# The last modulation section computed by VectorE during gate and up

## The chip, the cores and the metric

The program runs on one core of a Trainium2 chip. The metric is the device time of one execution in microseconds. Engines: TensorE (PE; its weight loads are PEld), VectorE (DVE), ScalarE (ACT), GpSimd (POOL) and SyncE (SP), which here only issues DMAs. All data are fp32.

## The reference, cut to what matters

One block of a diffusion backbone over 640 tokens (128 of a prompt, 512 of a sample), width 2048, hidden width 5632. Two condition vectors, one for each group of tokens, give six modulation sections of 2048 columns:

```python
mod_ctx = jax.nn.silu(c_ctx) @ w_ada[l] + b_ada[l]
mod_lat = (jax.nn.silu(c) @ w_ada[l] + b_ada[l])[:, None, :]
...
sh1, sc1, g1, sh2, sc2, g2 = jnp.split(mod, 6, axis=-1)
h = x * (1 + sc1) + sh1
m, s_f, s_b = mixer(h, ...)                     # w_in, heads, pooling, w_out
x = layer_norm(ALPHA * x + g1 * m, ln1_g, ln1_b)
h = x * (1 + sc2) + sh2
gate, up = jnp.split(h @ w_gu, 2, axis=-1)
f = (jax.nn.silu(gate) * up) @ w_down
x = layer_norm(ALPHA * x + g2 * f, ln2_g, ln2_b)
```

The last section, g2, is used only behind the down product.

## The kernel before

The stages follow one another: a first part with sections sh1 and sc1; 33 units of w_in, between which the four heads and the pooling run (to 753 us); w_out; gate and up (from 984 to 2095 us); down and the last norm.

**Precision.** Every large product is done as three matmuls: ScalarE rounds a weight to `w_hi` (L977, L1210, L1312), VectorE or GpSimd subtracts to get the rest `w_lo` (L1377, L1666, L956), and TensorE does hi*hi, hi*lo and lo*hi.

**Modulation.** The other four sections (16 MB of `w_ada` each) are computed between the units of w_in. A row of 512 columns is four steps of four matmuls (`ada_step`, L2011: condition of 32 columns as stationary operand, 512 weight columns moving, fp32). A written-out order (`make_schedule`) has 9 places `SLOT` and 2 places `INNER` in each of the four heads; `with_modulation` fills each with a pair of steps until the 64 are used, at the end of the third head. The two `INNER` lie between two groups of outer products. At the next `SLOT` a row is summed over the four partial results: `adasum` (L2191) for a section kept as rows in DRAM (`mod_d`), `adacol` (L2198) for one kept as columns.

**Gate and up.** A block b is 128 hidden columns of gate and of up. The two first blocks are plain; the other 42 are done by a scheme of seven products in place of eight. A product is 24 matmuls of 320 columns (L2278 to L2280), numbered n from 16 to 309; its seven weights, called items 0 to 6 here, are made of four quarters A11, A12, A21, A22 of 128 x 1024. GpSimd forms four sums in a row for a block (L942, L945, L948, L951); item 2 is the last of them, items 3, 4 and 6 the others, and 0, 1 and 5 are quarters as loaded. ScalarE rounds an item (L1210), VectorE takes the rest (the split, L1666, `prod_rest`), and TensorE uses it four products later (four weight buffers). Each engine's queue is written in the order of n: VectorE at n does the sums of the product before (`post`, L1839 to L1858, and L1822), then the split of item n - 1. SyncE loads a quarter of the next block as soon as the split that frees its buffer is done: A12 behind item 2, A11 behind item 3, A21 behind item 4, A22 behind item 5, and stores a finished block in between. GpSimd's first sum waits for A21 and A22; its third and fourth also wait for the splits of items 0 and 1.

Of the kernel before, what the change touches and what calls it, by code (L numbers as in the profile page):

```python
# [20 lines left out]
ALU = mybir.AluOpType  # L21
# [130 lines left out]

def prod_of(n):

    return PLAIN + (n - N_PLAIN) // 7, (n - N_PLAIN) % 7
# [14 lines left out]
ADA = [(2, "row", 0), (4, "col", SC), (3, "col", SH), (5, "row", 1)]  # L170
# [7 lines left out]
N_ADA = 16  # L178
# [49 lines left out]
def with_modulation(flat):  # L228


    out, done, behind = [], 0, []
    for item in flat:
# [4 lines left out]
        if done < ADA_STEPS:  # L237
            out += [("ada", done // 4, done % 4), ("ada", done // 4, done % 4 + 1)]
            done += 2
            last = done // 4 - 1 if done % 4 == 0 else None  # L240
# [81 lines left out]
def backbone(nc, x_all, state_gla, w_ada, w_in_b, wa2, w_pool_l, w_out, w_gu_b, w_down, consts,  # L322
# [62 lines left out]
    group_sum = cols(C_SUM, 2)  # L385
    mod_col = cols(C_MOD, 64).rearrange("p (s k c) -> p s k c", s=2, c=2)
# [221 lines left out]
    down_gates = sem("down_gates")  # L608
    down_filled = sem("down_filled")
# [46 lines left out]
    def _(sp):  # L656
# [144 lines left out]
        for i in range(2, N_OUT):  # L801
# [3 lines left out]
            if i == 4:  # L805
                for x in range(2):
                    sp.wait_ge(spilled[x], 16 * n_out[x])
                    sp.wait_ge(drained[x], FILLS[x])
                sp.wait_ge(row_out, 16 * 8)
                load_gates(0)  # L810
# [59 lines left out]
        def load_down_rows(nb):  # L870

            if nb == 0:
                for x in range(2):
                    sp.wait_ge(hid_out[x], 16 * FB // 2)
                sp.wait_ge(prod_done, N_PROD)
                sp.wait_ge(xn_out, 16 * TT)
            else:
                sp.wait_ge(down_evac, TT * nb)
# [10 lines left out]

        for b in range(PLAIN + 1, FB):  # L890
            load_quad(b + 1, A12)
            load_quad(b + 1, A11)
            if b == PLAIN + 1:
                store_hid(0)
            store_hid(b - 2)
            load_quad(b + 1, A21)
            load_quad(b + 1, A22)
        load_down(0)
# [62 lines left out]
    def _(act):  # L961
# [7 lines left out]
        def split_in(u):  # L969
# [5 lines left out]
            elif u >= 3:  # L975
# [6 lines left out]
                             ACT.Silu).then_inc(cond_ready, 1)  # L982

# [329 lines left out]

        for n in range(9, N_PROD):
            b, i = prod_of(n)
            if n > N_PLAIN and i == 1:
                act.wait_ge(prod_done, n)
                act.wait_ge(gated, 2 * b - 2)
                nc.scalar.activation(post_a(b), prod_bank(n - 1), ACT.Copy).then_inc(first_copy, 1)
            if n - 1 < N_ITEM:  # L1320
# [45 lines left out]
    def _(dve):  # L1366
# [492 lines left out]

        for n in range(9, N_PROD + 1):  # L1860
# [6 lines left out]
            if n - 1 < N_ITEM:  # L1867
                prod_rest(n - 1)
            if n == 12:
# [123 lines left out]
    def _(pe):  # L1993
# [332 lines left out]

        for n in range(N_PLAIN, N_PROD):
            pe.wait_ge(prod_split, n - 3)
# [117 lines left out]
```

## Time and profile before

| | us |
|---|---|
| median of 3 runs | 2719.36 (2711.6 to 2723.58) |
| the profiled execution | 2721.88 |
| its span | 2720.1 |
| TensorE busy | 2643.3 (97%) |
| VectorE busy | 1424.9 (52%) |
| ScalarE busy | 898.4 (33%) |
| GpSimd busy | 652.8 (24%) |

The span runs from the first to the last instruction in the trace. Busy shares are means over stages with different limits. Where TensorE is busy all the time, the matmuls themselves are the limit; for any other engine it matters when it ends what TensorE waits for, not how busy it is. In the rows a bracket behind an instruction gives the idle time ahead of it and what ended it.

### The profile page before, as it was taken

Reading aid. Unit: us, or ns where it says so; the run is one execution under the profiler, and the core shown is the slowest. Engines: PE = TensorE matmul, PEld = TensorE weight load, DVE = VectorE, ACT = ScalarE, POOL = GpSimd, SP = SyncE. Lnnn points to the kernel's source line nnn. Section 1 sums busy time; section 2 is a strip of 40 time slices with the busy share of each in tenths; the row PEclk is TensorE's granted clock in tenths of the full one; section 3 lists DMA queues with packets and bytes.
Section 4 is the critical chain, followed back from the end, with each engine's and each line's share of the span. In section 5 each row is a group of like instructions: output and inputs, shape, how many; then the busy total and the mean of one; then the engine's idle time right before and its main releaser. Section 6 shows DMA issues by size and latency. Waiting matters only on the chain.

```text
span 2720.1 us, 37395 instructions
## 1 busy us (share of the span) xinstructions
PE 2643.3 (97%) x16040; PEld 2354.7 (87%) x16040; DVE 1424.9 (52%) x1680; ACT 898.4 (33%) x940; POOL 652.8 (24%) x218
## 2 busy tenths in 40 slices
PE   5999999998999999999999999999999999999997
PEld 3787877797988879999999999999999888888875
DVE  5323232346576457655555545555566354444578
ACT  4333333332311154333333333333333333333343
POOL 0000000000000001344443444344434333333440
PEclk9999999999999989999999999999999999999998
DMA  9775757422463142332233323332334645464566
GB/s 378 281 277 209 272 207 255 153 90 91 176 218 118 64 159 80 108 108 88 93 108 108 96 86 106 108 103 84 101 108 158 239 174 213 174 213 166 208 231 233
DMA packets 179384, 438.11 MB, mean 161 GB/s; under 512 B 9980, under 2 KB 25732, under 8 KB 173076
## 3 DMA queue, kind: packets, MB, share of 16 engines
q1 hardware_dynamic: 176916, 430.48, 45.4%
q10 hardware_dynamic: 2304, 5.24, 0.5%
q8 instruction: 127, 2.08, 0.3%
q14 instruction: 37, 0.30, 0.0%
HBM read 401.83 MB, written 33.85 MB: 160 GB/s over the span
## 4 chain that ended last, share of the span: by engine, by line
PE 62%; DVE 11%; DMA 10%; POOL 10%; issue 4%; ACT 3%; SPq 0%; POOLq 0%; ACTq 0%; DVEq 0%
PE ps L2355 6%; PE ps L2356 6%; PE ps L2357 6%; DMA raw_w<-w_gu_b 5%; PE ps L2278 5%; PE ps L2280 5%; PE ps L2279 5%; PE ps L2031 5%; PE ps L2033 5%; PE ps L2032 5%; POOL raw_w L945 3%; PE ps L2011 3%; DVE w_lo L1666 3%; POOL low L942 2%; POOL raw_w L948 2%
## 5 line engine op out<-in xcount | busy, mean ns | idle before, releaser
L1666 DVE TENSOR_TENSOR w_lo<-raw_w,w_hi 128x1024 fp32r<-128x1024 f32 x264 | 336.6, 1276 | 297.6 <-ACT w_hi L1210 294.7
L1210 ACT ACTIVATE w_hi<-raw_w 128x1024 fp32r<-128x1024 f32 x264 | 270.1, 1054 | 601.0 <-POOL raw_w L951 368.9
L2278 PE MATMUL ps<-x_hi,w_hi 128*128 128x320 f32 x1408 | 435.7, 309 | 1.0 <-DVE w_lo L1666 0.7
L2279 PE MATMUL ps<-x_lo,w_hi 128*128 128x320 f32 x1408 | 435.1, 309 | 0.0
L2280 PE MATMUL ps<-x_hi,w_lo 128*128 128x320 f32 x1408 | 435.1, 309 | 0.0
L942 POOL TENSOR_TENSOR low<-raw_w 128x1024 f32<-128x1024 f32 x41 | 103.7, 2528 | 1098.8 <-DMA raw_w<-w_gu_b 1058.7
L1801 DVE TENSOR_TENSOR x_lo<-low,x_hi 128x2560 fp32r<-128x2560 f32 (+2 forms) x55 | 221.3, 4027 | 262.6 <-ACT x_hi L1303 262.6
L2355 PE MATMUL ps<-w_hi,x_hi 128*128 128x512 f32 x880 | 343.8, 391 | 7.7 <-DVE w_lo L1932 2.8
L2356 PE MATMUL ps<-w_lo,x_hi 128*128 128x512 f32 x880 | 343.1, 390 | 0.0
L2357 PE MATMUL ps<-w_hi,x_lo 128*128 128x512 f32 x880 | 342.9, 390 | 0.0
L2278 PE MATMUL ps<-low_r,w_hi 128*128 128x320 f32 x1072 | 333.0, 311 | 1.5 <-DVE w_lo L1666 1.5
L2279 PE MATMUL ps<-low_r,w_hi 128*128 128x320 f32 x1072 | 332.2, 310 | 0.0
L2280 PE MATMUL ps<-low_r,w_lo 128*128 128x320 f32 x1072 | 332.1, 310 | 0.0
L2031 PE MATMUL ps<-x_hi,w_hi 128*128 128x320 f32 x1024 | 322.9, 315 | 1.8 <-DVE x_lo L1434 1.8
L2033 PE MATMUL ps<-x_hi,w_lo 128*128 128x320 f32 x1024 | 316.6, 309 | 0.0
L2032 PE MATMUL ps<-x_lo,w_hi 128*128 128x320 f32 x1024 | 316.5, 309 | 0.0
L956 POOL TENSOR_TENSOR w_lo<-raw_w,w_hi 128x2048 fp32r<-128x2048 f32 x45 | 212.5, 4723 | 352.5 <-ACT w_hi L1312 352.5
L2278 PEld LDWEIGHTS ps<-x_hi,w_hi 128*128 128x128 f32 x1408 | 264.4, 188 | 1.8 <-DVE w_lo L1666 1.3
L2279 PEld LDWEIGHTS ps<-x_lo,w_hi 128*128 128x128 f32 x1408 | 264.4, 188 | 0.0
L2280 PEld LDWEIGHTS ps<-x_hi,w_lo 128*128 128x128 f32 x1408 | 264.3, 188 | 0.0
L1377 DVE TENSOR_TENSOR w_lo<-raw_w,w_hi 128x2048 fp32r<-128x2048 f32 x48 | 110.0, 2291 | 262.8 <-ACT w_hi L977 262.7
L1312 ACT ACTIVATE w_hi<-raw_w 128x2048 fp32r<-128x2048 f32 x55 | 105.4, 1916 | 380.6 <-PE ps L2357 364.5
(238 smaller groups left out, 4362.9 us busy)
## 6 DMA issues: line engine op xcount, KB each, us to landing
raw_w<-w_gu_b SPq DMA_DIRECT2D x180, 512.0 KB, 5.6
low<-w_ada SPq DMA_DIRECT2D x68, 1024.0 KB, 6.9
raw_w<-w_down SPq DMA_DIRECT2D x55, 1024.0 KB, 5.2
low<-hidden_scratch SPq DMA_DIRECT2D x33, 1280.0 KB, 6.0
raw_w<-w_in_b SPq DMA_DIRECT2D x33, 1024.0 KB, 9.1
x_raw<-w_ada SPq DMA_DIRECT2D x25, 1024.0 KB, 15.2
raw_w<-w_out SPq DMA_DIRECT2D x16, 1024.0 KB, 5.1
hidden_scratch<-high SPq DMA_DIRECT2D x44, 320.0 KB, 5.9
```

Of the source, the lines that this page charges most:

```text
L1210: nc.scalar.activation(weight(0, w), src, ACT.Copy).then_inc(prod_hi, 1)
L1666: nc.vector.tensor_tensor(weight(1, n), src, weight(0, n).bitcast(F32), ALU.subtract).then_inc(prod_split, 1)
L1801: nc.vector.tensor_tensor(hid_slot(x_lo, j), hid_raw(j), hid_slot(x_hi, j).bitcast(F32), ALU.subtract).then_inc(hid_split, 1)
L2031: mm(out, wh, xh, start=first, stop=False)
L2032: mm(out, wh, xl, start=False, stop=False)
L2033: ins = mm(out, wl, xh, start=False, stop=last)
L2278: mm(out, wh, version(v, 0, k), start=first and k == 0, stop=False)
L2279: mm(out, wh, version(v, 1, k), start=False, stop=False)
L2280: ins = mm(out, wl, version(v, 0, k), start=False, stop=last and k == HK - 1)
L2355: mm(ps[:, (i + 7) % 8, :], xh, rh, start=begin, stop=False)
L2356: mm(ps[:, (i + 7) % 8, :], xh, rl, start=False, stop=False)
L2357: ins = mm(ps[:, (i + 7) % 8, :], xl, rh, start=False, stop=end)
```

## The change

Section 5 (g2) is no longer among the sections done between the units of w_in: 12 rows and 48 steps are left of 16 and 64. Since every third `SLOT` is now left empty, they still end with the third head. Section 5 is computed during gate and up: 8 groups of 256 columns, each 16 steps (one for every 128 rows of `w_ada`), one step every second product. A step is a load of 128 x 256 into one buffer (L928 of the new kernel), and on VectorE, behind the split of that product, two instructions that add the loaded tile times the condition to two running sums (`late_step`; a scalar_tensor_tensor, L1947, or a tensor_scalar at a group's start, L1949). Every 34 products TensorE sums a group over the partitions with four small matmuls (`sum_late`, running sums as stationary operand, ones moving), ScalarE copies the result, and SyncE stores it with four DMAs of one column.

```diff
+def late_at(n):
+    q, at = divmod(n - LATE_FROM, LATE_GAP)
+    return (q, at) if n >= LATE_FROM and q < N_LATE else (N_LATE, 0)
+def late_step_of(n):
+    q, at = late_at(n)
+    return KT * q + at // 2 if q < N_LATE and at % 2 == 0 and at < 2 * KT else None
...
-ADA = [(2, "row", 0), (4, "col", SC), (3, "col", SH), (5, "row", 1)]
+ADA = [(2, "row", 0), (4, "col", SC), (3, "col", SH)]
+LATE, LATE_FROM, LATE_W, LATE_GAP = 5, 26, 256, 34
+N_LATE = D // LATE_W
...
-N_ADA = 16
+N_ADA = 12
...
-        if done < ADA_STEPS:
+        seen += item[1] == 0
+        if done < ADA_STEPS and (item == INNER or seen % 3):
...
+        def late_traffic(n):
+            i = late_step_of(n + 2)
+            if i is not None:
+                if i:
+                    sp.wait_ge(late_used, i)
+                else:
+                    sp.wait_ge(cond_late, 1)
+                at = LATE * D + LATE_W * (i // KT)
+                sp.dma_start(late_stage, w_ada[P * (i % KT):P * (i % KT) + P, at:at + LATE_W]).then_inc(late_in, 16)
+            q, at = late_at(n - 1)
+            if q < N_LATE and at == 2 * KT + 1:
+                sp.wait_ge(late_row_done, q + 1)
+                for c in range(2):
+                    for half in range(LATE_W // P):
+                        to = LATE_W * q + P * half
+                        j = 4 * c + 2 * half
+                        sp.dma_start(mod_d[1, c, to:to + P], late_row[:, j:j + 1]).then_inc(late_out, 16)
         for b in range(PLAIN + 1, FB):
+            n = ITEMS + 7 * (b - PLAIN)
             load_quad(b + 1, A12)
+            late_traffic(n - 4)
             load_quad(b + 1, A11)
+            late_traffic(n - 3)
...
             load_quad(b + 1, A21)
+            late_traffic(n - 2)
             load_quad(b + 1, A22)
+            for i in range(-1, 3):
+                late_traffic(n + i)
...
+        def late_act(n):
+            q, at = late_at(n)
+            if q < N_LATE and at == 2 * KT + 1:
+                act.wait_ge(late_sum, q + 1)
+                if q:
+                    act.wait_ge(late_out, 16 * 4 * q)
+                nc.scalar.activation(late_row, ps[:, (n + 4) % 8, HALF:HALF + 8], ACT.Copy).then_inc(late_row_done, 1)
...
+        def late_step(n):
...
+            q, k = divmod(i, KT)
+            dve.wait_ge(late_in, 16 * (i + 1))
...
+            for c in range(2):
+                acc, by = cols(late_acc[c], LATE_W), cond_now[:, k, c:c + 1]
+                if k:
+                    ins = nc.vector.scalar_tensor_tensor(acc, late_stage, by, acc, ALU.mult, ALU.add)
+                else:
+                    ins = nc.vector.tensor_scalar(acc, late_stage, by, None, ALU.mult)
+            ins.then_inc(late_used, 1)
...
             if n - 1 < N_ITEM:
                 prod_rest(n - 1)
+            late_step(n)
...
+        def sum_late(n):
+            q, at = late_at(n)
+            if q == N_LATE or at != 2 * KT:
+                return
+            pe.wait_ge(late_used, KT * (q + 1))
+            if q:
+                pe.wait_ge(late_row_done, q)
+            for j in range(4):
+                at = late_acc[j // 2] + P * (j % 2)
+                ins = mm(ps[:, (n + 5) % 8, HALF + 2 * j:HALF + 2 * j + 2], cols(at, P), cols(C_ONES, 2),
+                         start=True, stop=True)
+            ins.then_inc(late_sum, 1)
         for n in range(N_PLAIN, N_PROD):
+            sum_late(n)
```

TensorE in the heads, at the sixth `SLOT` of a head, before: the end of a group of products with the states (64x256), a pair of steps (32x512, eight matmuls), a column sum (128x2), the next unit.

```order
L2161 MATMUL ps<-low 64x256 x2
L2166 MATMUL ps<-low 64x256 x2
L2161 MATMUL ps<-low 64x256 x2
L2166 MATMUL ps<-low 64x256 x2
L2011 MATMUL ps<-low,perm 32x512 x8
L2198 MATMUL ps<-perm,high 128x2 x4
L2031 MATMUL ps<-x_hi,w_hi 128x320
```

And in the new order, at the same place:

```order
L2254 MATMUL ps<-low 64x256 x2
L2259 MATMUL ps<-low 64x256 x2
L2254 MATMUL ps<-low 64x256 x2
L2259 MATMUL ps<-low 64x256 x2
L2284 MATMUL ps<-high,perm 2x512
L2124 MATMUL ps<-x_hi,w_hi 128x320
L2125 MATMUL ps<-x_lo,w_hi 128x320
```

The pair is gone; which sum stands here has shifted, since rows now end at other places.

VectorE in gate and up, from the split of item 2 to that of item 5, before (L1666 the splits, the others sums on finished products):

```order
L1666 TENSOR_TENSOR w_lo<-raw_w,w_hi 128x1024
L1857 TENSOR_TENSOR high<-ps,high 128x320
L1858 TENSOR_TENSOR high<-ps,high 128x320
L1666 TENSOR_TENSOR w_lo<-raw_w,w_hi 128x1024
L1822 TENSOR_TENSOR high<-high 128x320
L1666 TENSOR_TENSOR w_lo<-raw_w,w_hi 128x1024
L1839 TENSOR_TENSOR high<-ps,high 128x320
L1666 TENSOR_TENSOR w_lo<-raw_w,w_hi 128x1024
```

The same in the new order, in every second block (L1732 the splits, L1947 the new step):

```order
L1732 TENSOR_TENSOR w_lo<-raw_w,w_hi 128x1024
L1947 SCALAR_TENSOR_TENSOR perm<-perm 128x256 x2
L1923 TENSOR_TENSOR high<-ps,high 128x320
L1924 TENSOR_TENSOR high<-ps,high 128x320
L1732 TENSOR_TENSOR w_lo<-raw_w,w_hi 128x1024
L1888 TENSOR_TENSOR high<-high 128x320
L1732 TENSOR_TENSOR w_lo<-raw_w,w_hi 128x1024
L1947 SCALAR_TENSOR_TENSOR perm<-perm 128x256 x2
L1905 TENSOR_TENSOR high<-ps,high 128x320
L1732 TENSOR_TENSOR w_lo<-raw_w,w_hi 128x1024
```

Two steps stand between the split of item 2 and that of item 5; in the blocks between these there is one, behind item 3.

## Rows read from the trace of the kernel before

**Rows 1.** The page, busy time of each engine: us, share of the span, instructions.

```profile
PE 2643.3 (97%) x16040; PEld 2354.7 (87%) x16040; DVE 1424.9 (52%) x1680; ACT 898.4 (33%) x940; POOL 652.8 (24%) x218
```

**Rows 2.** Busy us by stretch (PE, PEld, DVE, ACT, POOL; TensorE's clock, DMA share, GB/s).

```profile
270.00:520.00 250.00, 249.32 (x1807) 201.33 (x1807) 84.34 (x135) 82.90 (x106) 0.75 (x1) 1.00 0.67 239
1100.00:2060.00 960.00, 959.96 (x6546) 959.69 (x6545) 522.77 (x624) 325.47 (x390) 417.04 (x156) 1.00 0.31 100
```

**Rows 3.** Timeline of TensorE, a pair of modulation steps (start, us, what) and what follows.

```profile
514.80 1.92 PE L2011 MATMUL ps<-low,perm 128*32 128x512 f32 x16
516.65 0.70 PE L2072 MATMUL ps<-low 64*128 64x256 f32 x2
```

**Rows 4.** The same, a row sum and what follows, then four column matmuls.

```profile
531.26 1.02 PE L2191 MATMUL ps<-high,perm 128*2 128x512 f32 x2 [0.88 <-DVE low L1619]
532.21 0.41 PE L2031 MATMUL ps<-x_hi,w_hi 128*128 128x320 f32 x1
...
288.07 1.05 PE L2198 MATMUL ps<-perm,high 128*128 128x2 f32 x8
288.99 0.40 PE L2031 MATMUL ps<-x_hi,w_hi 128*128 128x320 f32 x1
```

**Rows 5.** Timelines of VectorE and TensorE at the scores of a head.

```profile
303.15 0.82 DVE L1553 TENSOR_TENSOR low<-low 128x640 f32<-128x640 f32 x1
...
306.39 0.80 PE L2126 MATMUL ps<-low 128*64 128x64 f32 x20
```

**Rows 6.** Timeline of VectorE over one block of gate and up.

```profile
1309.20 1.23 DVE L1666 TENSOR_TENSOR w_lo<-raw_w,w_hi 128x1024 fp32r<-128x1024 f32 x1 [6.01 <-ACT w_hi L1210]
...
1318.77 0.49 DVE L1842 TENSOR_TENSOR high<-ps,high 128x320 f32<-128x320 f32 x1 [1.20 <-PE ps L2280]
...
1325.81 0.49 DVE L1851 TENSOR_TENSOR high<-high,ps 128x320 f32<-128x320 f32 x1 [1.10 <-PE ps L2280]
1326.33 1.00 DVE L1854 TENSOR_TENSOR high<-high 128x320 f32<-128x320 f32 x1
1333.35 1.23 DVE L1666 TENSOR_TENSOR w_lo<-raw_w,w_hi 128x1024 fp32r<-128x1024 f32 x1 [6.02 <-ACT w_hi L1210]
...
1336.42 0.48 DVE L1822 TENSOR_TENSOR high<-high 128x320 f32<-128x320 f32 x1
1336.82 1.22 DVE L1666 TENSOR_TENSOR w_lo<-raw_w,w_hi 128x1024 fp32r<-128x1024 f32 x1
...
1338.36 1.22 DVE L1666 TENSOR_TENSOR w_lo<-raw_w,w_hi 128x1024 fp32r<-128x1024 f32 x1
...
1343.41 0.49 DVE L1842 TENSOR_TENSOR high<-ps,high 128x320 f32<-128x320 f32 x1 [1.20 <-PE ps L2280]
```

**Rows 7.** Timeline of GpSimd, its four sums and the next start.

```profile
1321.21 2.42 POOL L942 TENSOR_TENSOR low<-raw_w 128x1024 f32<-128x1024 f32 x1 [13.20 <-DVE w_lo L1666]
1323.77 3.21 POOL L945 TENSOR_TENSOR raw_w<-raw_w 128x1024 f32<-128x1024 f32 x1
...
1329.75 2.41 POOL L951 TENSOR_TENSOR raw_w<-raw_w 128x1024 f32<-128x1024 f32 x1
1345.71 2.41 POOL L942 TENSOR_TENSOR low<-raw_w 128x1024 f32<-128x1024 f32 x1 [13.55 <-DMA raw_w<-w_gu_b]
```

**Rows 8.** Timelines of ScalarE (rounding) and SyncE (the last two quarters).

```profile
1332.26 2.01 ACT L1210 ACTIVATE w_hi<-raw_w 128x1024 fp32r<-128x1024 f32 x2 [8.90 <-POOL raw_w L951]
...
1338.07 1.86 SPq L827 DMA_DIRECT2D raw_w<-w_gu_b  x2
```

**Rows 9.** A group of VectorE by form: count, busy us, mean ns, idle before.

```profile
L1593 DVE SCALAR_TENSOR_TENSOR low<-low,perm,ps 128x256 f32<-128x256 f32 x56 | 26.9, 480 | 1.7
```

**Rows 10.** DMA issues: count, KB each, median us to landing.

```profile
raw_w<-w_gu_b SPq DMA_DIRECT2D x180, 512.0 KB, 5.6
low<-state_gla SPq DMA_DIRECT2D x8, 128.0 KB, 6.9
low<-w_pool_l SPq DMA_DIRECT2D x4, 256.0 KB, 3.0
```

More of the change, by code:

```diff
@@ L228, in with_modulation @@
 def with_modulation(flat):
-    out, done, behind = [], 0, []
+    out, done, behind, seen = [], 0, [], 0
     for item in flat:
@@ L385, in backbone @@
     group_sum = cols(C_SUM, 2)
+    late_acc = [C_COND + LATE_W * c for c in range(2)]
+    late_stage = cols(C_VEC, LATE_W)
+    cond_now = cols(C_VEC + LATE_W, 32).rearrange("p (k c) -> p k c", c=2)
+    late_row = cols(C_VEC + LATE_W + 32, 8)
     mod_col = cols(C_MOD, 64).rearrange("p (s k c) -> p s k c", s=2, c=2)
@@ L608, in backbone @@
     down_gates = sem("down_gates")
+    cond_late = sem("cond_late")
+    late_in = sem("late_in")
+    late_used = sem("late_used")
+    late_sum = sem("late_sum")
+    late_row_done = sem("late_row_done")
+    late_out = sem("late_out")
     down_filled = sem("down_filled")
@@ L808, in _ @@
                     sp.wait_ge(drained[x], FILLS[x])
-                sp.wait_ge(row_out, 16 * 8)
+                sp.wait_ge(row_out, 16 * 4)
                 load_gates(0)
@@ L876, in load_down_rows @@
                 sp.wait_ge(xn_out, 16 * TT)
+                sp.wait_ge(late_out, 16 * 4 * N_LATE)
             else:
@@ L982, in _ @@
                              ACT.Silu).then_inc(cond_ready, 1)
+        act.wait_ge(cond_ready, 1)
+        nc.scalar.activation(vec(V_COND, 32), vec(V_COND, 32), ACT.Silu).then_inc(cond_ready, 1)
         def in_rooted(t):
@@ L1319, in _ @@
                 nc.scalar.activation(post_a(b), prod_bank(n - 1), ACT.Copy).then_inc(first_copy, 1)
+            late_act(n)
             if n - 1 < N_ITEM:
@@ L1858, in post @@
                 nc.vector.tensor_tensor(a, prod_bank(m), a, ALU.add).then_inc(posted, 1)
+        def late_step(n):
+            if n == LATE_FROM - 4:
+                dve.wait_ge(cond_ready, 2)
+                dve.wait_ge(folded_s, 2 * HK)
+                dve.wait_ge(folded_v, 2 * HK)
+                nc.vector.tensor_copy(cond_now, vec(V_COND, 32).rearrange("p (k c) -> p k c", c=2)).then_inc(cond_late, 1)
+            i = late_step_of(n)
+            if i is None:
+                return
+            q, k = divmod(i, KT)
+            dve.wait_ge(late_in, 16 * (i + 1))
+            if i:
+                dve.wait_ge(late_used, i)
+            else:
+                dve.wait_ge(cond_late, 1)
+            if q and not k:
+                dve.wait_ge(late_sum, q)
+            for c in range(2):
+                acc, by = cols(late_acc[c], LATE_W), cond_now[:, k, c:c + 1]
+                if k:
+                    ins = nc.vector.scalar_tensor_tensor(acc, late_stage, by, acc, ALU.mult, ALU.add)
+                else:
+                    ins = nc.vector.tensor_scalar(acc, late_stage, by, None, ALU.mult)
+            ins.then_inc(late_used, 1)
         for n in range(9, N_PROD + 1):
@@ L2325, in bank_free @@
                 pe.wait_ge(posted, 4 * (b - PLAIN) + max(1, i - 2))
+        def sum_late(n):
+            q, at = late_at(n)
+            if q == N_LATE or at != 2 * KT:
+                return
+            pe.wait_ge(late_used, KT * (q + 1))
[6 more added lines that the diff above has]
+            ins.then_inc(late_sum, 1)
         for n in range(N_PLAIN, N_PROD):
+            sum_late(n)
             pe.wait_ge(prod_split, n - 3)
```

## The prediction

> **What bounds the kernel now.** I read the page's busy times first, then the busy times by stretch, then the waits, and then the timeline of each engine over one block of gate and up. TensorE is busy 2643 of 2720 us [rows 1]: a matmul taken from it counts in full wherever it has no idle time. It has none in the two stretches that the change touches: 249.3 of 250 us while the heads are computed, and 959.96 of 960 us in gate and up, at full granted clock [rows 2]. So time taken from TensorE in the first stretch is gained, and what is put into the second costs nothing only as long as nobody there gets later than TensorE.
>
> How late they are now is the question. In gate and up a block of seven products takes TensorE 24.64 us: the same VectorE sum, released by TensorE, stands at 1318.77 and 1343.41 [rows 6]. Beside it runs a second cycle, of the weights. When the split of item 5 is done (1338.36 + 1.22 = 1339.58), SyncE issues the last quarter of the next block (the second issue of its row, at 1339.60) [rows 6, 8]. It lands and GpSimd starts its four sums at 1345.71, 6.13 us later [rows 7]. In the block before they ran from 1321.21 to 1332.16, 10.95 us [rows 7]. ScalarE rounds item 2 from 1332.26 and VectorE splits it from 1333.35 to 1334.58 [rows 6, 8]; the splits of items 3, 4 and 5 and the sums between them stand in its queue right behind, without a gap, up to 1339.58. From split to split of item 2 that is 1333.35 - 1309.20 = 24.15 us, and from sums to sums 1345.71 - 1321.21 = 24.50 [rows 6, 7]. The cycle of the weights is thus as long as TensorE's, 0.1 to 0.5 us shorter. Its reserve: item 2, done at 1334.58, is wanted by the product that starts three products after the one that ended at 1325.8, so at 1325.8 + 3 x 3.52 = 1336.3, 1.7 us later [rows 6]. The busy shares hide this: VectorE is busy only 523 of the 960 us [rows 2].
>
> **The change, part by part.** The sum is made against the profiled execution (span 2720.1, time 2721.9 us), 2.5 us above the median of 2719.4.
>
> *Taken out of the heads.* 16 steps of matmuls go, which stand in pairs: a pair takes from 514.80 to 516.65, 1.85 us [rows 3]; 8 x 1.85 = 14.8. Four sums of a row go, each 531.26 to 532.21, 0.95 us [rows 4]: 3.8. Together 18.6 us. Pairs leave the third, sixth and ninth slot of each head, so something could come late that they had covered. The tightest place is the scores: VectorE ends its last factor at 303.97 and TensorE uses it from 306.39 [rows 5], 2.4 us of room against 1.85 taken out ahead of it. The pairs between the two groups of outer products stay. I cost exposed waits at 0, at most 8 x 1 us. The 16 MB read less here free DMA queues for which TensorE doesn't wait: nothing.
>
> *Put on TensorE.* Eight times, four small fp32 matmuls. The same form takes 288.07 to 288.99, 0.92 us [rows 4]: 7.4 us if TensorE is never waiting, and nothing where it waits in every block anyway. Each also waits for the last VectorE step, two products earlier. That step stands behind a split that only the product after this one needs, so it can hold TensorE by up to a product (3.5 us); the seven blocks around then run on the reserve so won. I put 3 us on it.
>
> *Put on VectorE.* 128 steps of two instructions of 256 columns, one step every second product, behind a split. The trace shows no such operation with both inputs in SBUF. With one in PSUM 256 columns take 480 ns [rows 9]; a plain product of 320 columns in SBUF keeps the queue for 1336.82 - 1336.42 = 0.40 us [rows 6], 0.32 for 256. I take 0.375 each, nearer to the row of the same memory, 0.75 for a step. Of TensorE's 7.04 us for two products that is little. For the weights' cycle it is not: of its 24.15 us, the stretch from the split of item 2 to that of item 5 is queue order on VectorE, and alternately two steps (behind items 2 and 4) or one (behind item 3) fall in it. So 1.5 steps a block, +1.1 us (0.95 to 1.45).
>
> *GpSimd's sums.* While GpSimd works, VectorE's operations with two SBUF inputs are not free: the 320-column product that took 0.48 at 1336.42, with GpSimd idle, took 1.00 at 1326.33, and the sum that GpSimd started at 1323.77 took 3.21 in place of 2.41 [rows 6, 7]. One waits for the other to finish. Each step puts two more such operations, about one to two steps in a block beside the sums: each may hold GpSimd for its own 0.3 us and itself wait up to 2.4, behind which a split then waits. I take +0.5 us on the 10.95 (0 to 1.4). The Trainium skill (GPSIMD Engine Reference, Key points) says that GpSimd shares its SBUF interfaces with VectorE and contends with instructions that have two SBUF inputs. The new accumulation is of that kind; by a rule that spared it, this term would be 0 and the sum some 19 us lower.
>
> *DMAs.* 128 loads of 128 KB (rows of 1 KB) go through SyncE's queue, one or two of them ahead of the last quarter. 256 KB landed in 3.0 us on a quiet queue, 128 KB in 6.9 on a crowded one [rows 10]. At the mean rate of the quarters' burst they are a few tenths each, part of which the quarter spends in the queue already. +0.3 us a block (0 to 0.6). The 32 stores of a column are 4 issues every 34 products: left out.
>
> *The sum.* The weights' cycle becomes 24.15 + 1.1 + 0.5 + 0.3 = 26.05 us, 1.41 over TensorE's 24.64. The steps run over products 26 to 294, 38 blocks: 38 x 1.41 = 53.6, less the reserve of 1.7, plus the 3 of the small matmuls: 55. So 2721.9 - 18.6 + 55 = 2758; from the median 2756. I take 2754, since the whole +1.1 may be partly made up where the last quarter only waits in the queue. Ends: 0.95 + 0 + 0 gives 25.1 and 38 x 0.46 - 1.7 = 16, so 2719. At the other, 24.15 + 1.45 + 1.4 + 0.6 = 27.6 and 38 x 2.96 - 1.7 = 111, so 2814.
>
> **Rivals.**
> *The cover holds.* If the cycle of the weights has more give than I see (a late split is made up by a shorter stay of the quarter in the queue), TensorE stays full: 2721.9 - 18.6 + 7.4 = 2710.7, from the median 2708. For it: TensorE did not wait once in 960 us [rows 2], and VectorE is nearly half idle. Against: the splits of items 2 to 5 stand without a gap [rows 6].
> *The cycle grows by little.* At the low end above the two halves cancel: 2719, no change. It decides at 0.5 us over TensorE's block (18.6 / 38).
> *VectorE waits for its own loads.* A step's load is issued when the step before is done, and has one buffer. If it lands as the crowded one did, the chain load, step, issue is 6.9 + 0.75 + 0.5 = 8.15 against the 7.04 of two products; all of VectorE then goes at that pace: 128 x 1.1 = 141, so 2842 from the median. The point is a landing of 5.8 us. For it: two of the loads in a block are issued behind a quarter, and quarters land in 5.6 [rows 10]. Against: others find the queue empty.
> *The front gives nothing.* If the pairs only covered waits, the 18.6 stay and the time is 2773. Against: the last head runs its scores without them.
>
> **How the numbers follow.** A measurement of this kernel tells from no change about 0.5%: 2706 to 2733. Forecast (the weights' cycle over TensorE's by more than 0.9 us) 0.60; cover holds 0.12; grows by little 0.15; VectorE waits for its loads 0.08; nothing from the front 0.05. The forecast's own range is 2733 to 2800. Faster by over 0.5%: part of the cover case, 0.07. Same: the rest of it and most of the little growth, 0.19. Slower: 0.74. The range for 8 in 10 is 2714 to 2805.
>
> **What would show it.** The head stretch ends 18 us earlier with TensorE still full: the first part. In gate and up TensorE should show an idle gap in nearly every block of those 38, ended by a VectorE split, ahead of the product that uses item 2; the distance between GpSimd's first sums should be 25.5 to 26.5 us, and back at 24.64 in the last blocks, where no steps are left. GpSimd's sums should take 11.2 to 12 us. I am wrong if TensorE is full in gate and up, or if VectorE's longest wait there is for the 128 KB loads.

## The result, and the profile after

| | us |
|---|---|
| before, median of 6 runs | 2719.49 (2711.6 to 2723.58) |
| after, median of 6 runs | 2816.97 (2813.18 to 2822.0) |
| ratio | 1.0362, 95% interval 1.0343 to 1.0381 |
| span of the profiled execution after | 2816.7 |
| forecast | 2754, range 2714 to 2805 |

The change costs 97.5 us, 3.6%. Slower was forecast, but by 35 us, and 2817 lies above the range.

The page of after: busy time by engine, and its line on DMA packets.

```profile
PE 2666.0 (95%) x15968; PEld 2382.0 (85%) x15968; DVE 1755.6 (62%) x1937; ACT 892.1 (32%) x941; POOL 650.5 (23%) x218
...
DMA packets 193964, 438.15 MB, mean 156 GB/s; under 512 B 16372, under 2 KB 48508, under 8 KB 187652
```

TensorE has 72 instructions fewer than before and is busy longer, 2666 us against 2643 [rows 1]. Work was taken off it and the span grew by 97 us, so it must wait, run at a lower clock, or both. The windows of [rows 2] in the trace of after say where (the columns are those of that group):

```profile
270.00:520.00 250.00, 248.69 (x1799) 206.15 (x1798) 89.07 (x140) 82.00 (x103) 0.75 (x1) 1.00 0.55 197
1100.00:2060.00 960.00, 894.09 (x5914) 885.28 (x5913) 764.97 (x793) 290.55 (x357) 368.99 (x141) 0.97 0.38 105
```

The heads look as before. In gate and up TensorE is busy 894 us of 960 where it was busy 959.96, and its mean granted clock is 0.97 instead of 1.00 [rows 2]. One line of the program in both traces gives the length of the stage, a matmul of the first product of gate and up and of others (count, ns min/median/max, first and last start):

```profile
L2278 PE MATMUL ps<-low_r,w_hi x1072: 305/309/633, 984.4 to 2092.5; 128*128 128x320 f32 x179
```

```profile
L2371 PE MATMUL ps<-low_r,w_hi x1072: 302/309/637, 972.2 to 2191.6; 128*128 128x320 f32 x179
```

The first is of before, the second of after. The stage begins 12.2 us earlier, which is what everything ahead of it gave, and takes 1219.4 us from first to last start where it took 1108.1: 111.3 more. The waits in that stage of after, by engine and line (us in total, times, longest):

```profile
PE ps L2371 <- DVE w_lo L1732: 46.1, 25, 8.9
PE ps L2430 <- DVE perm L1947: 24.5, 7, 6.3
PE ps L2373 <- issue: 3.1, 2, 1.6
```

```profile
DVE perm L1947 <- DMA perm<-w_ada: 115.6, 41, 15.9
DVE w_lo L1732 <- ACT w_hi L1266: 92.4, 77, 8.6
```

L2371 is the product, L2430 the small matmuls, L1732 the splits and L1947 the new step. TensorE waits 46.1 us ahead of products and 24.5 us ahead of seven of the eight groups of small matmuls, 73.7 us with the third row. The small matmuls themselves take 0.91 us a group at full clock, up to the next product's start, as forecast (0.92, so 7.4 for eight). The other 30 of the 111 fit the clock: over the stage its mean is 0.973 where it was 0.998 before, and the difference, taken of 1219 us, is 30. One wait shows how it comes about, a group of small matmuls that had waited 6.29 us, and then the windows ahead of and behind that wait (the column after the five engines is the granted clock):

```profile
1204.36 1.87 PE L2430 MATMUL ps<-perm 128*128 128x2 f32 x8 [6.29 <-DVE perm L1947]
```

```profile
1204.00:1212.00 8.00, 7.64 (x38) 7.64 (x38) 4.72 (x8) 3.01 (x6) 0.02 (x1) 0.65 0.43 110
1190.00:1198.00 8.00, 8.00 (x56) 7.80 (x54) 6.80 (x7) 1.06 (x1) 5.34 (x2) 1.00 0.12 41
```

TensorE was full at 2.4 GHz, waited, and then ran for some us at 1.2 GHz: 38 matmuls in 8 us instead of 56, and 1.87 us for the eight instructions that took 1.05 before [rows 4]. And VectorE's longest wait, 15.9 us, is for the 128 KB loads, which the prediction had named as the sign that it is wrong.

The waits are not spread evenly. GpSimd's first sum of a block gives the length of a block (first and last start of its 41):

```profile
L996 POOL TENSOR_TENSOR low<-raw_w x41: 2340/2547/3468, 1064.9 to 2156.4; 128x1024 f32<-128x1024 f32 x41
```

That is 1091.5 / 40 = 27.3 us a block against 24.6. Of the 40 distances 31 are 24.0 to 27.1 us, 25.5 in the mean; nine are 28.2 to 40.8. In four of the five longest (34.9 to 40.8) the excess lies between the split of item 5 and GpSimd's next sum. This is SyncE at the first of them, then what the profile tells of the load issued at 1344.65 (count, KB, us to landing), then VectorE and GpSimd:

```profile
1342.24 0.33 SPq L928 DMA_DIRECT2D perm<-w_ada  x1
1342.61 2.00 SPq L936 DMA_DIRECT2D gates_scratch<-perm  x4
1344.65 0.43 SPq L854 DMA_DIRECT2D raw_w<-w_gu_b  x1
...
raw_w<-w_gu_b SPq DMA_DIRECT2D x1, 512.0 KB, 13.4
```

```profile
1355.26 0.88 DVE L1947 SCALAR_TENSOR_TENSOR perm<-perm 128x256 f32<-128x256 f32 x2 [8.59 <-DMA perm<-w_ada]
...
1356.98 1.22 DVE L1732 TENSOR_TENSOR w_lo<-raw_w,w_hi 128x1024 fp32r<-128x1024 f32 x1
```

```profile
1332.40 2.40 POOL L1005 TENSOR_TENSOR raw_w<-raw_w 128x1024 f32<-128x1024 f32 x1 [1.16 <-DVE w_lo L1732]
1358.20 2.41 POOL L996 TENSOR_TENSOR low<-raw_w 128x1024 f32<-128x1024 f32 x1 [23.40 <-DVE w_lo L1732]
```

The last quarter stands right behind the four column stores (L936) and lands after 13.4 us; the median is 5.6 [rows 10]. That is at 1358.1, and GpSimd starts at 1358.20. Its row names another releaser, a split, which ends at 1356.98 + 1.22 = 1358.20 too: that split stood behind a step which had waited 8.59 us for its own load, issued at 1342.24. So both of the things that GpSimd waits for are held up by transfers that met the column stores.

### The profile page after: what moved, and what is told of

The parts are those of the page before. It is cut to its first block and busy times, and to the rows that moved or that the text cites. A ratio compares the mean times of both kernels' runs of the same rounds, so it can differ in the third digit from the quotient of the medians.

```text
span 2816.7 us, 37780 instructions
## 1 busy us (share of the span) xinstructions
PE 2666.0 (95%) x15968; PEld 2382.0 (85%) x15968; DVE 1755.6 (62%) x1937; ACT 892.1 (32%) x941; POOL 650.5 (23%) x218
## 5 line engine op out<-in xcount | busy, mean ns | idle before, releaser
L2371 PE MATMUL ps<-x_hi,w_hi 128*128 128x320 f32 x1408 | 443.1, 315 | 23.7 <-DVE w_lo L1732 23.2
L1732 DVE TENSOR_TENSOR w_lo<-raw_w,w_hi 128x1024 fp32r<-128x1024 f32 x264 | 406.2, 1540 | 82.4 <-ACT w_hi L1266 78.2
L996 POOL TENSOR_TENSOR low<-raw_w 128x1024 f32<-128x1024 f32 x41 | 110.0, 2683 | 1190.3 <-DMA raw_w<-w_gu_b 1153.0
L2371 PE MATMUL ps<-low_r,w_hi 128*128 128x320 f32 x1072 | 339.0, 316 | 22.8 <-DVE w_lo L1732 22.8
L2372 PE MATMUL ps<-low_r,w_hi 128*128 128x320 f32 x1072 | 336.5, 314 | 0.0
L1947 DVE SCALAR_TENSOR_TENSOR perm<-perm 128x256 f32<-128x256 f32 x240 | 251.8, 1090 | 120.3 <-DMA perm<-w_ada 115.6
L2124 PE MATMUL ps<-x_hi,w_hi 128*128 128x320 f32 x1024 | 323.4, 316 | 1.8 <-DVE x_lo L1500 1.8
L2371 PEld LDWEIGHTS ps<-x_hi,w_hi 128*128 128x128 f32 x1408 | 268.5, 191 | 31.9 <-DVE w_lo L1732 29.6
```

The costliest lines, as they stand in the source:

```text
L1732: nc.vector.tensor_tensor(weight(1, n), src, weight(0, n).bitcast(F32), ALU.subtract).then_inc(prod_split, 1)
L1947: ins = nc.vector.scalar_tensor_tensor(acc, late_stage, by, acc, ALU.mult, ALU.add)
L2124: mm(out, wh, xh, start=first, stop=False)
L2371: mm(out, wh, version(v, 0, k), start=first and k == 0, stop=False)
L2372: mm(out, wh, version(v, 1, k), start=False, stop=False)
```

## The experiments

The kernel before was run beside every group of them, with medians of 2718.4 to 2719.4, so times of different groups can differ by 1 us for that reason alone. Where rows of a run are shown, line numbers are that kernel's own.

**Stores of rows.** The ones become stationary (32 columns) and the running sums moving, so that a sum lies in a row; four stores of 512 B take the place of four stores of 128 x 4 B. All else is the changed kernel, but the small matmuls have another form.

```diff
-                ins = mm(ps[:, (n + 5) % 8, HALF + 2 * j:HALF + 2 * j + 2], cols(at, P), cols(C_ONES, 2),
+                ins = mm(ps[32 * j:32 * j + 32, (n + 5) % 8, HALF:HALF + P], cols(C_ONES, 32), cols(at, P),
...
-                        sp.dma_start(mod_d[1, c, to:to + P], late_row[:, j:j + 1]).then_inc(late_out, 16)
+                        sp.dma_start(mod_d[1, c:c + 1, to:to + P], late_row[j:j + 1, :]).then_inc(late_out, 16)
```

> The changed kernel with one thing altered: the eight groups are summed with ones as stationary and the running sums as moving operand, so that a result lies along a row and its four stores have one piece of 512 bytes each in place of 128 pieces of 4 bytes. Theory S (the column stores hold up the DMA queue, and the quarter behind them lands 8 to 13 us late, eight times): 2817 - 8 x 8 = about 2750, with no quarter landing later than 9 us, and GpSimd's distances between blocks all between 25 and 27 us. Theory L (VectorE's steps and its waits for their 128 KB loads lengthen every block): 2800 to 2817. Theory C (the four small matmuls and their wait for VectorE cost most): 2810 to 2817, as they are as many as before.

Measured: 2750.75 us, ratio 1.0117 (1.0097 to 1.0138). The edit gives 2816.97 - 2750.75 = 66 us, two thirds of the loss and more. No quarter lands later than 9 us. About 6 of the 66 us are the small matmuls: as rows a group takes 0.43 us at full clock (the row below, of the run with steps alone and the later sum) where it took 1.05 [rows 4]. Over the eight groups, some of them at the lower clock, they push the products back by 5.0 us where it was 10.8. The other 60 go with the stores.

```profile
1180.25 0.43 PE L2431 MATMUL ps<-perm 128*32 128x128 f32 x8
```

TensorE's waits here:

```profile
PE ps L2430 <- DVE perm L1947: 23.9, 7, 6.2
PE ps L2371 <- DVE w_lo L1732: 9.6, 13, 1.5
```

The waits ahead of products have nearly gone (46.1 to 9.6); those ahead of the small matmuls have not.

**Column stores in the kernel before.** 32 stores of 128 x 4 B from constants into a scratch tensor, at the same places; no steps, no loads, section 5 computed as before.

```diff
+                        sp.dma_start(col_d[c, to:to + P], vec(V_COND + j, 1)).then_inc(late_out, 16)
```

> The kernel before, with nothing added but the 32 column stores, at the same places of SyncE's queue as in the changed kernel, from constants into a scratch tensor; the modulation stays where it was. Theory S: each of the eight groups makes a quarter 8 to 13 us late, less the reserve of 1.7: 8 x 8 = 64, so 2719 + 64 = 2784, and a lower granted clock behind each stall. Theories L and C: 2719 to 2722.

Measured: 2765.63 us, ratio 1.0168 (1.0145 to 1.019). They cost 46 us by themselves: six of the 40 distances between GpSimd's first sums are 31 to 39 us. Beside the steps they cost about 60. VectorE's wait for the steps' loads, 115.6 us in after and 65.9 with stores of rows, is a likely part of the difference.

**The front alone.** No loads, steps, sums and stores; section 5 is not computed, and the down stage uses the rows of section 2.

> The changed kernel without any of the work added in gate and up: no loads, steps, small matmuls or stores, so that section 5 is not computed (the down stage multiplies by section 2 in its place). It measures what the heads gain alone. By the prediction's term: 2719.4 - 18.6 = 2701. By the changed kernel's trace (w_out started 11.8 us earlier, of which 2.65 us were lost before the first row was reached): 2704 to 2708.

Measured: 2704.34 us, ratio 0.9942 (0.9925 to 0.9959). The work taken out gives 14.9 us, 3.7 fewer than the 18.6 forecast. Of these 0.8 show: TensorE's waits for `w_ada` in the first part, 21.5 us before, are 22.3 here (23.7 in after). The rest was not followed up.

At this point the forecast seemed right but for the stores: its sum without them, 2754, and the run with rows, 2751, agree. The next runs showed that they agree by accident.

**The sum one product later.** The kernel with stores of rows; the small matmuls stand three products behind the last step instead of two. The edit moves something else too: the first step stands at product 21 in place of 26, and a group comes every 35 products in place of 34. Since 35 is five blocks of seven, the small matmuls now meet the same place of a block every time, ahead of the fourth of its seven products.

```diff
-LATE, LATE_FROM, LATE_W, LATE_GAP = 5, 26, 256, 34
+LATE, LATE_FROM, LATE_W, LATE_GAP = 5, 21, 256, 35
...
-            if q == N_LATE or at != 2 * KT:
+            if q == N_LATE or at != 2 * KT + 1:
```

> The kernel with stores of rows (2750.8), with the small matmuls one product later, so that VectorE's last step before them is a product older; nothing else moves. Theory W (what is left is the cycle of the weights, 25.7 us a block against TensorE's 24.6): TensorE's 23.9 us of waits at the small matmuls (7 of them) are time that it would have waited elsewhere; they turn up as waits for the splits, and the time is 2742 to 2752. Theory N (the small matmuls' own wait for VectorE is the cost): the 23.9 us go and the time is about 2727.

Measured: 2736.02 us, ratio 1.0069 (1.0054 to 1.0085). TensorE no longer waits there at all, its waits for splits go from 9.6 to 20.7 us, and 14.7 us are gained: between the two theories, neither of which gave this time. How much of it is the later product and how much the new place isn't separated. In the kernel with stores of rows the eight groups stood at different places, and TensorE's waits were 6.2, 1.9, 0, 1.6, 1.3, 2.6, 4.6 and 5.7 us; the 1.3 belong to the place that all eight have now. An estimate from this one value: the place alone would leave 8 x 1.3 = 10 of the 23.9 us.

**Loads alone, steps alone.** Two halves of the kernel with stores of rows. In the first each step works on 2 of its 256 columns and leaves out the other 254; in the second one load takes the place of 128, and all steps use that tile.

> The kernel with stores of rows, its 128 loads of 128 KB kept, but each step multiplies and adds 2 of its 256 columns and leaves out the other 254. Theory W with the steps' own time and their meeting GpSimd's sums as the cause: the block is back at 24.6 to 24.8 us, VectorE's wait for the loads is harmless and the time is 2709 to 2718 (2704.3 of the shortened front plus 7.4 for the small matmuls). Rival D (the loads' place in SyncE's queue and VectorE's waits for them, 70 us, are the cause): the block stays above 25.3 us and the time at 2735 or more.

> The kernel with stores of rows, with one load in place of 128: all steps run at full width, on the same tile, so that no step waits for a transfer and none stands in SyncE's queue; 127 loads are left out. Theory W with the steps' own time as the cause: still 25.4 us a block or more, 2738 to 2750. Rival D: about 24.7 us a block and 2711 to 2720.

Measured: loads alone 2734.70 us, ratio 1.0063 (1.005 to 1.0077); steps alone 2719.88, ratio 1.0002 (0.9993 to 1.0011). Both sides go against theory W, which is the mechanism of the forecast; rival D gave 2735 or more for the first and 2711 to 2720 for the second. Full-width steps without loads cost 15.5 us over the front alone, and narrow steps with loads cost 30.4; both still have the waits at the small matmuls (9.9 and 10.7 us). VectorE's waits for the loads in the first of the two:

```profile
DVE perm L1947 <- DMA perm<-w_ada: 96.6, 57, 3.3
```

**Steps alone, later sum.** The second half again, with the small matmuls a product later (127 loads are left out).

> The kernel with stores of rows and the later sum, with one load in place of 128 (127 are left out, all steps work on one tile): the steps at full width alone, without a wait for a load and without a hold at the small matmuls. If the steps' own length in the stretch from item 2 to item 5 lengthened the weights' cycle as forecast (+1.1 +0.5 us), the block is 25.3 us or more and the time 2735 or more. If the quarter's stay gives all of it back, the block is 24.64 to 24.8 and the time 2709 to 2717.

Measured: 2709.46 us, ratio 0.9967 (0.9955 to 0.9979). This is 5.1 us over the front alone. The small matmuls, as rows, account for 8 x 0.45 = 3.6 of it (what a group adds between two products). So 128 steps at full width cost 1.5 us, which is nothing that can be measured here, at the very places where the forecast let them and GpSimd's sums lengthen the weights' cycle by 38 x 1.6 = 61 us.

**Loads ordered earlier.** The kernel with stores of rows and the later sum, with all its loads, and a second buffer.

```diff
-    late_stage = cols(C_VEC, LATE_W)
+    late_stage = [cols(C_VEC, LATE_W), cols(P, LATE_W)]
...
-            i = late_step_of(n + 2)
+            first = late_step_of(n + 2)
+            for i in [] if first is None else [0, 1] if first == 0 else [first + 1]:
...
-                    sp.wait_ge(late_used, i)
+                    sp.wait_ge(late_used, i - 1)
```

> The kernel with stores of rows and the later sum (2736.0), with a second buffer: each load is ordered one step earlier, when the step before the last is done; the 128 loads, their bytes and their place in SyncE's queue stay. Theory X (VectorE's wait for a load of one buffer, 61.5 us there, pushes the splits back): the wait falls under 15 us and the time to 2712 to 2722. Rival Y (the loads delay the quarters behind them on the queue, wherever they are waited for): the quarter's stay stays near 5.4 us, the block near 25.4 and the time at 2730 or more.

Measured: 2716.83 us, ratio 0.9992 (0.9983 to 1.0001). VectorE doesn't wait for a load any more. The 19.2 us came from the wait for one buffer, not from the loads' place in the queue; the last quarter stays 5.43 us in the mean, as rival Y had it, and this costs nothing. How 61.5 us of waits on VectorE, the longest 2.6, come to cost anything shows in one block of the kernel with one buffer, VectorE and then GpSimd:

```profile
1342.70 4.99 DVE L1947 SCALAR_TENSOR_TENSOR perm<-perm 128x256 f32<-128x256 f32 x2 [0.54 <-DMA perm<-w_ada]
1347.62 0.48 DVE L1913 TENSOR_TENSOR high<-ps,high 128x320 f32<-128x320 f32 x1
1348.02 3.02 DVE L1732 TENSOR_TENSOR w_lo<-raw_w,w_hi 128x1024 fp32r<-128x1024 f32 x1
```

```profile
1342.46 2.40 POOL L996 TENSOR_TENSOR low<-raw_w 128x1024 f32<-128x1024 f32 x1 [14.15 <-DMA raw_w<-w_gu_b]
1345.00 2.41 POOL L999 TENSOR_TENSOR raw_w<-raw_w 128x1024 f32<-128x1024 f32 x1
...
1351.12 2.41 POOL L1005 TENSOR_TENSOR raw_w<-raw_w 128x1024 f32<-128x1024 f32 x1 [1.16 <-DVE w_lo L1732]
```

The step's two instructions take 0.88 us when GpSimd is idle and 4.99 here: they start 0.24 us into GpSimd's first sum and end at 1347.69, behind the end of its second (1347.41). The split behind them takes 3.02 instead of 1.22, ends at 1351.04, and GpSimd's fourth sum had waited 1.16 for it. A load that is half a microsecond late puts the step beside the sums, and the delay comes back to GpSimd. Over the stage, grouped by form (busy us, mean ns of one, idle before), with one buffer and then with two:

```profile
L1732 DVE TENSOR_TENSOR w_lo<-raw_w,w_hi 128x1024 fp32r<-128x1024 f32 x262 | 412.7, 1576 | 67.5 <-ACT w_hi L1266 66.9
L1947 DVE SCALAR_TENSOR_TENSOR perm<-perm 128x256 f32<-128x256 f32 x240 | 242.4, 1051 | 61.8 <-DMA perm<-w_ada 61.5
```

```profile
L1734 DVE TENSOR_TENSOR w_lo<-raw_w,w_hi 128x1024 fp32r<-128x1024 f32 x262 | 370.2, 1414 | 195.7 <-ACT w_hi L1268 194.3
L1949 DVE SCALAR_TENSOR_TENSOR perm<-perm 128x256 f32<-128x256 f32 x240 | 172.1, 759 | 0.0
```

The mean of one instruction of a step falls from 1051 to 759 ns, and VectorE's slack (its wait for ScalarE) grows from 67 to 194 us. The Trainium skill (SBUF — State Buffer, "SBUF: two separate sides") says that the pair of ports shared by VectorE and GpSimd is an exclusive lock, held for the whole instruction, and counts a VectorE instruction with two SBUF inputs among those that take it. The rows agree: 0.44 us for one of the two when alone, about 2.5 when it starts beside a 2.4 us sum.

The kernel with two buffers shows why the length of the steps costs nothing. VectorE from the split of item 2 to that of item 5, with two steps between; SyncE's issue of the last quarter; GpSimd's first sums:

```profile
1348.52 1.23 DVE L1734 TENSOR_TENSOR w_lo<-raw_w,w_hi 128x1024 fp32r<-128x1024 f32 x1 [6.00 <-ACT w_hi L1268]
...
1355.11 1.23 DVE L1734 TENSOR_TENSOR w_lo<-raw_w,w_hi 128x1024 fp32r<-128x1024 f32 x1
```

```profile
1356.37 0.33 SPq L854 DMA_DIRECT2D raw_w<-w_gu_b  x1
```

```profile
1336.40 2.42 POOL L998 TENSOR_TENSOR low<-raw_w 128x1024 f32<-128x1024 f32 x1 [13.60 <-DMA raw_w<-w_gu_b]
...
1360.36 2.69 POOL L998 TENSOR_TENSOR low<-raw_w 128x1024 f32<-128x1024 f32 x1 [13.03 <-DMA raw_w<-w_gu_b]
```

The stretch is 1356.34 - 1348.52 = 7.82 us; before it was 1339.58 - 1333.35 = 6.23 [rows 6]. But GpSimd starts 1360.36 - 1356.34 = 4.02 us behind it, where it took 6.13 [rows 6, 7], and this block is 23.96 us long: it gives back more than the whole. That is one block. The means over all 40 blocks, worked out from the timelines of each kernel, say how it goes in general. The four parts make up a block; the fourth, from the last sum to the split of item 2, is 1.2 us in all of them.

| mean over 40 blocks, us | GpSimd's four sums | from the split of item 2 to that of item 5 | then to the next sums | block |
|---|---|---|---|---|
| before | 11.13 | 6.23 | 6.08 | 24.63 |
| front alone | 11.03 | 6.23 | 6.15 | 24.60 |
| steps alone, later sum | 10.97 | 7.34 | 5.32 | 24.81 |
| all loads, later sum, two buffers | 10.97 | 7.34 | 5.43 | 24.93 |
| all loads, later sum, one buffer | 11.42 | 7.38 | 5.43 | 25.42 |
| stores of rows (39 blocks) | 11.59 | 7.74 | 5.27 | 25.79 |
| after | 11.51 | 8.17 | 6.43 | 27.29 |

The steps lengthen the stretch by 1.11 us, as forecast. The stay of the last quarter gives 0.76 of it back, and GpSimd's sums 0.16. It gives the more the later the quarter is ordered: with steps alone the stay is 5.68 us in the mean in the 24 blocks with one step in the stretch (7.02 us) and 4.77 in the 16 with two (7.81). The landings say why. Before, three DMAs are still under way when the last quarter is issued; the quarter ahead of it needs another 4.57 us, and the last one lands 1.36 us after all of them. In the blocks with two steps the quarter ahead needs only another 2.81 us, and the last one lands 1.76 us after all of them. So most of the 6.08 us is time spent behind other transfers, and that part gives way. The table also places the cost of one buffer: of its 0.49 us a block 0.45 stand in GpSimd's sums.

**Column stores from another queue.** The changed kernel, its 32 column stores issued by ScalarE behind its copy instead of by SyncE.

```diff
+                        nc.scalar.dma_start(mod_d[1, c, to:to + P], late_row[:, j:j + 1]).then_inc(late_out, 16)
```

> The changed kernel (2817) with its 32 column stores issued by ScalarE into its own queue, behind the copy, instead of by SyncE; the loads of the quarters and of the steps stay on SyncE's. Theory Q (what stalls is the queue in which they stand): the quarters pass them and the time is that of stores of rows, 2750 to 2757. Theory E (their 512 packets hold the DMA engines for every queue): the four long blocks stay, 2790 to 2817.

Measured: 2814.75 us, ratio 1.0341 (1.0321 to 1.036), the same as from SyncE's queue within the intervals; six of the 40 distances are 34 to 42 us. What stalls is not the queue in which they stand. The Trainium skill (DMA: Bandwidth & Descriptors, "Issuing engines are not separate DMA queues") says that issuing from several engines saves only the time of issuing; this run agrees.

**Wide stores in the kernel before.** The kernel before with 32 stores of 128 packets each, as in the second run, but 512 B a packet in place of 4.

```diff
-                        sp.dma_start(col_d[c, to:to + P], vec(V_COND + j, 1)).then_inc(late_out, 16)
+                        sp.dma_start(col_d[2 * c + half], cols(C_TRI, P)).then_inc(late_out, 16)
```

> The kernel before with 32 stores added at the places of the column stores, as in the run with column stores from constants (2765.6, ratio 1.0168), with the same 128 packets each, but of 512 B in place of 4 B: 64 KB a store. Theory 4 B (packets that small are what the DMA engines are slow on): no long block, TensorE's waits as before, 2717 to 2725. Rival N (the number of packets behind one another on the queue is the cost): the blocks with 14 to 20 us between the split of item 5 and the first sum stay, 2755 or more.

Measured: 2718.12 us, ratio 1.0003 (0.9991 to 1.0015). The load issued right behind four such stores (KB, us to landing), with 4 B packets and then with 512 B:

```profile
raw_w<-w_gu_b SPq DMA_DIRECT2D x1, 512.0 KB, 13.0
column_scratch<-perm SPq DMA_DIRECT2D x1, 0.5 KB
```

```profile
raw_w<-w_gu_b SPq DMA_DIRECT2D x1, 512.0 KB, 5.9
column_scratch<-perm SPq DMA_DIRECT2D x1, 64.0 KB, 5.3
```

No quarter takes longer than 9 us to land. 128 times the bytes in as many packets cost nothing, so the number of packets is not the cause, and their size is, or what comes with it: the 4 B packets of a store also lie side by side in one stretch of 512 B in DRAM, and each wide packet fills 512 B of its own, which isn't separated here. The Trainium skill (DMA: Bandwidth & Descriptors, Specifications) gives 512 B as the least size for the full rate and says that the DMA does a read-modify-write below it. The pair agrees with the 512 B; no run shows the read-modify-write itself. The traces' packets add that the stores' own packets are short, 9 ns at the median for 4 B. Long are packets of other transfers: of those with 512 B or more, between 1000 and 2200 us, 87 took over 2.5 us with the column stores in the kernel before, 159 in after and 137 with ScalarE's queue, up to 10.4 us each, and none in the kernel before, with stores of rows or with wide stores. The packets of a quarter take 159 ns at the median.

**Other places for the steps, a candidate.** Stores of rows, two buffers, loads ordered two steps ahead, and the steps behind the splits of items 5, 6, 1 and every second time 0. Then the same with the later sum (and 0 two times in three, so that the steps end in time).

> A candidate: stores of rows, two buffers for the loads and loads ordered two steps ahead behind the last quarter's issue, and the steps moved off the stretch from the split of item 2 to that of item 5 (they stand behind the splits of items 5, 6, 1 and every second time 0). Theory W: the stretch is back at 6.2 us, the block at 24.64, and the time is 2704.3 + 7.4 = 2709 to 2714, 0.2 to 0.4% below the kernel before. Rival G (VectorE and GpSimd hold each other wherever the steps stand, since now nearly all of them meet GpSimd's sums): the sums of GpSimd grow from 11 to 12 us or more, block 25.2 us or more, 2725 or more.

Measured: 2722.04 us, ratio 1.0013 (1.0004 to 1.0022). TensorE waited 8.4 us at two of the small matmuls.

> The candidate again (stores of rows, two buffers, steps off the stretch between the splits of items 2 and 5; 2722.0), with the small matmuls one product later, three behind the last step. The 12.9 us in which TensorE waited there, 8.4 of them in two small matmuls, and most of the 7.5 us of half clock that follow such waits should go: 2704.3 + 7.4 = 2712, 2709 to 2715. If the meeting with GpSimd's sums is what is left instead, TensorE's waits turn up at the splits and the time stays at 2719 or more.

Measured: 2714.40 us, ratio 0.9979 (0.997 to 0.9988). TensorE's waits in the stage:

```profile
PE ps L2386 <- DVE w_lo L1747: 5.9, 7, 1.5
PE ps L2445 <- DVE perm L1962: 2.5, 3, 1.0
```

It is the best complete version, 4 us below before and 103 below the change as made. One instruction of its steps takes 1256 ns in the mean, since nearly all meet GpSimd's sums, and yet it is no slower than the kernel with two buffers and the old places (2716.8). Its block is 24.89 us: the stretch is back at 6.23, but the last quarter, ordered earlier again, stays 6.22, and the sums take 11.25. The places matter little.

## Why the prediction was wrong

The medians make a ladder. Its uncertainty is 3 to 7 us a rung from the intervals of the two ends, and in another order the rungs could come out differently (the column stores cost 46 us in the kernel before). Two rungs hold a second effect, told above: the later sum also has a new place, and the stores of rows come with shorter matmuls. The forecast's column is the sum of the prediction, 2758 from the profiled execution; it took 2754 from the median.

| part | forecast, us | measured, us | from |
|---|---|---|---|
| work taken out of the heads | -18.6 | -14.9 | front alone - before |
| small matmuls, steps and GpSimd's sums, nothing waited for | +61, less 19 and 1.7; small matmuls 0 | +5.1 | steps alone, later sum - front alone |
| the 128 loads, landed in time | +11 | +7.4 | loads ordered earlier - steps alone, later sum |
| VectorE's wait for one buffer | 0 | +19.2 | later sum - loads ordered earlier |
| TensorE's wait at the small matmuls | +3 | +14.7 | stores of rows - later sum |
| column stores | 0 | +66.2 | after - stores of rows |
| sum | +36 | +97.7 | |

The 19 are 38 x 0.49 us, by which the prediction had the weights' cycle shorter than TensorE's (24.15 against 24.64). The measured rungs add up to 97.7 and not 97.5, since the front alone is taken against the kernel before beside it (2719.25).

**The heads.** The mechanism was right, the size a quarter too large (18.6 against 14.9).

**"The 32 stores of a column are 4 issues every 34 products: left out."** This step failed, with the largest sum. The issues were counted, not the packets: four stores are 512 packets of 4 B, and the page gave [rows 10] only for transfers with rows of 1 KB and more. Nothing in the trace of before bounded them, and an unbounded term was set to zero instead of widening the range. What the runs showed in its place: 66 us from the edit that takes the column stores away, about 60 without the shorter matmuls, and 46 from the same stores alone in the kernel before. Without this term the changed kernel would have been inside the range, at 2751.

**"The cycle of the weights is thus as long as TensorE's."** This step failed too. The steps' +1.1 us and GpSimd's +0.5 a block were added to a cycle that was taken as rigid. It was not. The +1.1 was right, 1.11 measured; the stay of the last quarter in the queue, 6.13 us, was read as a duration, and it was mostly time behind other transfers, which shrinks when the quarter is ordered later. The start of the sum was misread as well: 24.15 us is the distance in one block, and the mean over 40 is 24.63, TensorE's own, so there were no 0.49 us to spare; what gave way was the stay. That the forecast, 2754, and the run with stores of rows, 2751, agree is luck: about 40 us for the steps, of which 5 were measured, make up for 3 us for the two waits, of which 34 were measured (19.2 and 14.7). The rival "the cover holds", with a chance of 0.12, was right on this point; it named this very give. The observation against it, the splits without a gap, was true and did not matter.

**The sign that was found.** Products do wait for splits (25 times), and GpSimd's four sums took 11.5 us a block as forecast (11.13 before), but the waits came from the loads and stores: with both removed and the later sum, the steps still in VectorE's queue, TensorE was busy 958 of 960 us.

```profile
1100.00:2060.00 960.00, 958.11 (x6558) 953.45 (x6557) 764.21 (x870) 323.34 (x398) 402.04 (x154) 1.00 0.30 100
```

That row is of the run with steps alone and the later sum.

**The rival on loads** had the right wait (115.6 us in after) and a wrong law: it let all of VectorE go at the pace of load, step, issue. VectorE has slack, and with stores of rows and the later sum 61.5 us of waits cost 19.2, through the meeting with GpSimd's sums, not through its pace.

**The wait at the small matmuls** was seen ("behind a split that only the product after this one needs") and priced once, at 3 us, though it comes up to eight times: seven times in after, 24.5 us.

**TensorE's clock** was left out: about 30 of the 111 us in gate and up go with matmuls at 1.2 GHz behind waits of several us. A sum over waits alone comes out short by that.

Still open: why four column stores make packets of other transfers take up to 10 us, beyond the size of their own; where 2.9 of the 3.7 us missing in the heads went; how the 14.7 us divide between the later product and the new place; and what the 7.4 us of the loads in time consist of.

## What to carry to other kernels

Count a store by its packets and their bytes, not by its issues: with 4 B each a neighbour of theirs landed in 13 us instead of 6, and laying the result out in a row even shortened the matmuls that make it. Before adding work to a cycle, ask which of its parts is a wait in a queue, since that part gives way, and take its length from many blocks, not from one. A wait that is added needs a distance in the program: one more buffer (19 us) and one more product between producer and consumer, at a better place of the block (15 us together), turned a loss into no loss here.

## What the runs showed of the hardware that was not expected

- Four stores of 128 packets of 4 B held back loads on the same and on another queue, though their own packets took 9 ns; the same stores with 512 B a packet (64 KB each) landed in 3.0 to 6.4 us and held back none.
- A 256-column multiply-add of VectorE with both inputs in SBUF takes 0.48 us alone and up to 2.64 us when GpSimd is at a sum; in the block shown a start late by 0.5 us put two of them beside its sums.
- The load of a quarter, 512 KB, has no duration of its own in this kernel: from the split of item 5 to GpSimd's start it is 6.08 us in the mean before, and 4.77 in the blocks where it was ordered 1.6 us later in the cycle.
